# Two transformer blocks on one core: shift section behind the first taps, joined roots of two norms, another order of head pairs

## The reference

```python
sh1, sc1, g1, sh2, sc2, g2 = ada_terms(cond_lat, ada_w[i], ada_b[i])   # silu(c) @ w + b, six sections of 1024
hl = modulate(rmsnorm(x, norm1_g[i]), sh1, sc1)
yl = short_conv_mixer(hl, conv_w_in[j], conv_w[j], conv_w_out[j], True)
x = x + g1 * yl
x = x + g2 * swiglu(modulate(rmsnorm(x, norm2_g[i]), sh2, sc2), ffn_w_in[i], ffn_w_out[i])
return rmsnorm(x, final_g)
```

```python
h = _swiglu(_rmsnorm(x, g[0]), ...);  x = x + 0.5 * _rmsnorm(h, g[1])
h = mixer(_rmsnorm(x, g[2]));         x = x + _rmsnorm(h, g[3])
h = _swiglu(_rmsnorm(x, g[4]), ...);  x = x + 0.5 * _rmsnorm(h, g[5])
```

## Time and profile before

| | |
|---|---|
| median of 3 runs | 1320.87 us (1317.85 to 1321.43) |
| profiled execution, its own time | 1321.67 us |
| its span, first to last instruction | 1319.8 us |
| busy: DVE, ACT, POOL | 59%, 52%, 11% |
| mean TensorE clock granted | 0.994 of full |
| HBM read | 249.77 MB, 190 GB/s over the span |
| chain that ended last, by engine | PE 89%, DVE 4%, ACT 2% |

### The profile page before, as it was taken

How to read it: one execution, slowest core, us unless ns; L and a number is a source line. 1 busy time by engine, 2 the same in 40 slices (tenths; PEclk the granted TensorE clock), 3 DMA queues, 4 the chain that set the end, 5 groups by cost and what they waited for, 6 DMA issues and landing times.

```text
span 1319.8 us, 18568 instructions
## 1 busy us (share of the span) xinstructions
PE 1291.3 (98%) x6815; PEld 1064.7 (81%) x6815; DVE 781.8 (59%) x1023; ACT 687.9 (52%) x1035; POOL 139.5 (11%) x126
## 2 busy tenths in 40 slices
PE   8989999999999999999999999999999999999997
PEld 7877788887788888877888888888887897788886
DVE  4485666444755555666755556655556676755554
ACT  4453544444644445646644446544446656744443
POOL 3080097001600000020000000000000100000000
PEclk9999999999899999999999999999999999999999
DMA  9996386555455556572555554655563543555561
GB/s 338 378 373 207 123 302 213 188 183 186 160 179 184 182 187 215 171 205 64 189 184 184 184 202 157 209 183 184 188 225 126 162 151 119 189 186 183 183 205 57
DMA packets 177379, 253.64 MB, mean 192 GB/s; under 512 B 9352, under 2 KB 143796, under 8 KB 177332
## 3 DMA queue, kind: packets, MB, share of 16 engines
q1 hardware_dynamic: 174368, 244.33, 55.2%
q0 software_dynamic: 2624, 8.48, 1.7%
q10 hardware_dynamic: 340, 0.18, 0.1%
HBM read 249.77 MB, written 1.05 MB: 190 GB/s over the span
## 4 chain that ended last, share of the span: by engine, by line
PE 89%; DVE 4%; ACT 2%; DMA 1%; SPq 1%; POOL 1%; issue 1%; DVEq 0%; ACTq 0%; POOLq 0%
PE ps L598 26%; PE ps L600 25%; PE ps L599 25%; PE ps L638 2%; PE ps L639 2%; PE ps L683 2%; PE ps L646 2%; POOL arena L2198 1%; PE ps L1008 1%; PE ps L622 1%; DVE arena L1915 1%; DMA arena<-in_ada_w 1%; DMA raw<-in_conv_w_in 1%; PE ps L880 1%; SPq L477 1%; PE ps L869 1%
## 5 line engine op out<-in xcount | busy, mean ns | idle before, releaser
L1646 DVE TENSOR_TENSOR w_lo<-raw,w_hi 128x2048 fp32r<-128x2048 f32 x111 | 263.6, 2375 | 168.5 <-ACT w_hi L1182 168.5
L598 PE MATMUL ps<-w_lo,xT_hi 128*128 128x512 f32 x836 | 332.8, 398 | 3.0 <-DVE act_pair L1800 3.0
L600 PE MATMUL ps<-w_hi,xT_lo 128*128 128x512 f32 x836 | 327.5, 392 | 0.0
L599 PE MATMUL ps<-w_hi,xT_hi 128*128 128x512 f32 x836 | 327.2, 391 | 0.0
L1651 DVE SCALAR_TENSOR_TENSOR w_lo<-raw,par,w_hi 128x512 fp32r<-128x512 f32 x336 | 230.9, 749 | 135.1 <-ACT w_hi L1187 135.0
L1182 ACT ACTIVATE w_hi<-raw 128x2048 fp32r<-128x2048 f32 x111 | 212.1, 1912 | 143.6 <-PE ps L600 140.1
L1187 ACT ACTIVATE w_hi<-raw,par 128x512 fp32r<-128x512 f32 x336 | 214.3, 712 | 0.8 <-PE ps L600 0.8
L598 PEld LDWEIGHTS ps<-w_lo,xT_hi 128*128 128x128 f32 x836 | 157.8, 189 | 35.6 <-DVE act_pair L1800 3.5
L600 PEld LDWEIGHTS ps<-w_hi,xT_lo 128*128 128x128 f32 x836 | 157.7, 189 | 33.7
L599 PEld LDWEIGHTS ps<-w_hi,xT_hi 128*128 128x128 f32 x836 | 158.0, 189 | 31.6 <-issue 0.2
L598 PE MATMUL ps<-w_lo,hT_hi 128*128 128x512 f32 x400 | 156.7, 392 | 0.0
(11 more groups left out here) (248 smaller groups left out, 1527.6 us busy)
## 6 DMA issues: line engine op xcount, KB each, us to landing
raw<-in_ffn_w_gate SPq DMA_DIRECT2D x88, 512.0 KB, 3.7
raw<-in_ffn_w_up SPq DMA_DIRECT2D x88, 512.0 KB, 4.6
raw<-in_ffn_w_down SPq DMA_DIRECT2D x88, 512.0 KB, 4.0
raw<-in_ffn_w_in SPq DMA_DIRECT2D x44, 512.0 KB, 4.6
raw<-in_conv_w_in SPq DMA_DIRECT2D x24, 512.0 KB, 9.1
raw<-in_fox_w_in SPq DMA_DIRECT2D x24, 512.0 KB, 4.4
raw<-in_ffn_w_out SPq DMA_DIRECT2D x22, 512.0 KB, 4.1
raw<-in_ab_w_in SPq DMA_DIRECT2D x14, 512.0 KB, 4.4
```

What stands on the lines that cost most here:

```text
L598: pe.matmul(o, a_hi, b_lo, start=first, stop=False, skip_group_check=True)
L599: pe.matmul(o, a_hi, b_hi, start=False, stop=False, skip_group_check=True)
L600: return pe.matmul(o, a_lo, b_hi, start=False, stop=last, skip_group_check=True)
L1646: dve.tensor_tensor(w_lo[:, slot_of(n), :], raw[:, slot_of(n), :], w_hi[:, slot_of(n), :].bitcast(F32), ALU.subtract).then_inc(raw_done, 1)
```

## The change

There are three parts, in three places of the program.

**First mixer.** POOL's first load of the shift section waits for `evac_v` 2, that is for DVE's `conv_out(0)`. ACT multiplies the pieces later: `split(n + 7)`, `middle_taps(0)`, `split(n + 8)`, `conv_hi(0)` and `split(n + 9)` now stand ahead of `ada_times(0)`. On DVE `conv_out(0)` stands behind `split(n + 8)`. PE runs `shift_columns` behind units 10 and 11 and `mod_piece(6)`.

The diff, without the new semaphores and the lines that only rename; the lines of the orders above are left out:

```diff
@@ PE, AB @@
+            pair_part(n + 6, 0, 5)
             pe.wait_ge(evac_a, 9)
             pe.wait_ge(k_landed, 32)
             scores(AB, 0)
             scores(AB, 1)
-            pair_part(n + 6, 0, 5)
             pair_part(n + 6, 1, 5)
-            turn_probs(AB, 0)
             pe.wait_ge(tap_w_ok, 1)
             pe.wait_ge(rep_landed, 256)
             long_conv(0)
+            turn_probs(AB, 0)
+            long_conv(1, (0, TAPM // 2))
             head_outputs(AB, 0)
             turn_probs(AB, 1)
-            long_conv(1)
+            long_conv(1, (TAPM // 2, TAPM))
...
             turn_probs(AB, 3)
+            pe.wait_ge(oT_ok, 3)
+            down_part(n + 8, yT_hi, yT_lo, 6, 0, False, False, ks=(0,))
             head_outputs(AB, 3)
...
             pe.wait_ge(oT_ok, 4)
-            down_part(n + 8, yT_hi, yT_lo, 6, 0, False, False)
+            down_part(n + 8, yT_hi, yT_lo, 6, 0, False, False, ks=(1,))
@@ ACT, between(FFN0) @@
+                def summed_square(t):
+                    c = 2 * FINAL_EVENT + t
+                    act.wait_ge(x_mid, 2 * t + 2)
+                    act.activation(tmp[:, t, :], x[:, t, :], ACT.Square, scale=D ** -0.5,
+                                   accum_out=stat[:, 0, c:c + 1]).then_inc(x_sq, 1)
+                def gained_square(t):
+                    c = 2 * x_event(s) + t
+                    act.wait_ge(gained, t + 1)
+                    act.wait_ge(x_sq, 2 * FINAL_EVENT + t + 1)
+                    act.activation(tmp[:, t, :], xn[:, t, :], ACT.Square, scale=D ** -0.5,
+                                   accum_out=stat[:, 0, c:c + 1]).then_inc(gain_sq, 1)
...
-                        after(0)
+                        summed_square(0)
+                        gained_square(0)
                         split(n + 1)
                         turned_hi(s, 1)
-                        after(1)
-                        before(0)
-                        before(1)
+                        summed_square(1)
+                        gained_square(1)
+                        c, f = 2 * x_event(s), 2 * FINAL_EVENT
+                        act.wait_ge(x_sq, f + 2)
+                        act.activation(stat[:, 1, f:f + 2], stat[:, 0, f:f + 2], ACT.Sqrt, bias=eps[:, 0:1]).then_inc(x_std, 2)
+                        act.wait_ge(both_sq, 1)
+                        act.activation(stat[:, 1, c:c + 2], stat[:, 2, c:c + 2], ACT.Sqrt).then_inc(x_std, 2)
@@ DVE @@
+            def joined_roots():
+                c, f = 2 * x_event(FFN1), 2 * FINAL_EVENT
+                dve.wait_ge(x_sq, f + 2)
+                dve.wait_ge(gain_sq, 2)
+                link(dve.tensor_scalar(stat[:, 1, c:c + 2], stat[:, 0, f:f + 2], EPS, EPS * EPS, ALU.mult, ALU.add))
+                dve.tensor_tensor(stat[:, 2, c:c + 2], stat[:, 1, c:c + 2], stat[:, 0, c:c + 2], ALU.add).then_inc(both_sq, 1)
+                dve.wait_ge(x_std, f + 2)
+                dve.reciprocal(stat[:, 2, f:f + 2], stat[:, 1, f:f + 2]).then_inc(x_rstd, 2)
+                dve.wait_ge(x_std, c + 2)
+                dve.reciprocal(stat[:, 2, c:c + 2], stat[:, 1, c:c + 2]).then_inc(x_rstd, 2)
...
-            conv_out(0)
             split(n + 8)
+            conv_out(0)
@@ POOL @@
             pool.wait_ge(mod_ps, 4)
-            load_ada_p(0)
-            load_ada_p(1)
             pool.memset(half_sum, 0.0).then_inc(sum_cleared, 1)
             pool.wait_ge(sum_cleared, 2)
             sum_rows(half_sum, GATE1)
+            pool.wait_ge(evac_v, 2)
+            load_ada_p(0)
+            load_ada_p(1)
...
+            for t in range(TOKT):
+                pool.wait_ge(x_mid, 2 * t + 2)
+                pool.tensor_tensor(xn[:, t, :], x[:, t, :], rows[:, 1, :], ALU.mult).then_inc(gained, 1)
+
             pool.wait_ge(ada_ps, 5)
-            pool.wait_ge(x_new, x_count(CONV, 0, 0))
+            pool.wait_ge(x_rstd, 2 * x_event(FFN1) + 2)
```

More of the change, by code:

```diff
@@ L311, in block_program @@
         x_mid = sem("x_mid")
+        gained = sem("gained")
+        gain_sq = sem("gain_sq")
+        both_sq = sem("both_sq")
         gain_ok = sem("gain_ok")
@@ L1002, in _, with long_conv @@
             pair_part(n + 5, 1, 4)
-            def long_conv(c):
-                for m in range(TAPM):
+            def long_conv(c, ms=(0, TAPM)):
+                for m in range(*ms):
                     for q in range(4):
@@ L1434, in _ @@
             gate_out(0)
-            ada_times(0)
             split(n + 7)
             middle_taps(0)
-            ada_times(1)
             split(n + 8)
             conv_hi(0)
+            split(n + 9)
+            ada_times(0)
+            ada_times(1)
+            split(n + 10)
+            gate_out(1)
+            split(n + 11)
             ada_times(2)
-            split(n + 9)
-            gate_out(1)
+            middle_taps(1)
+            split(n + 12)
             ada_times(3)
-            split(n + 10)
-            split(n + 11)
+            split(n + 13)
+            conv_hi(1)
             act.wait_ge(ada_ps, 2)
             act.activation(mod[:, 0, :], ps[:, 1, 0:KT], ACT.Copy).then_inc(ada_row_a, 1)
-            middle_taps(1)
-            split(n + 12)
-            split(n + 13)
-            conv_hi(1)
             split(n + 14)
@@ L1703, in residual @@
                     o.then_inc(x_mid if b == FFN0 else x_new, 1)
+            def joined_roots():
[8 more added lines that the diff above has]
+                dve.reciprocal(stat[:, 2, c:c + 2], stat[:, 1, c:c + 2]).then_inc(x_rstd, 2)
             def final_x(t):
-                r = rms_x(FINAL_EVENT, t)
+                f = 2 * FINAL_EVENT + t
                 for h in range(2):
                     c = slice(h * 512, (h + 1) * 512)
-                    dve.scalar_tensor_tensor(x[:, t, c], x[:, t, c], r, rows[:, 1, c], ALU.mult, ALU.mult).then_inc(x_new, 1)
-            def joined_root(t):
-                c, f = 2 * x_event(FFN1) + t, 2 * FINAL_EVENT + t
-                dve.wait_ge(x_std, c + 1)
-                link(dve.reciprocal(stat[:, 0, c:c + 1], stat[:, 1, c:c + 1]))
-                dve.tensor_tensor(stat[:, 2, c:c + 1], stat[:, 0, c:c + 1], stat[:, 2, f:f + 1], ALU.mult).then_inc(x_rstd, 1)
+                    dve.tensor_scalar(x[:, t, c], xn[:, t, c], stat[:, 2, f:f + 1], None, ALU.mult).then_inc(x_new, 1)
             def norm_x(s, t):
@@ L1764, in between @@
                     residual(b, 1)
-                    final_x(0)
                     turned_lo(s, 1)
-                    final_x(1)
-                    for t in range(TOKT):
-                        joined_root(t)
+                    split(n + 1)
+                    joined_roots()
                 elif s in FOLDED:
@@ L1779, in between @@
                     residual(b, 1)
-                if s < 8:
+                if s < 8 and b != FFN0:
                     split(n + 1)
@@ L1818, in ffn @@
                 chunk(0)
+                if s == FFN1:
+                    for t in range(TOKT):
+                        final_x(t)
                 if s == FFN2:
@@ L1942, in _ @@
             outer_taps(0)
+            split(n + 8)
             conv_out(0)
-            split(n + 8)
             conv_lo(0)
```

18 lines of the change are left out of this document (8 added, 10 removed).

## The result

The changed kernel takes 1325.97 us, median of 5 runs (1324.08 to 1327.55), against 1320.87 us before. Its ratio to before is 1.0039, 95% interval 1.0027 to 1.0051, so it is slower by about 5 us. Medians and ratios here leave out two slow executions, one of the kernel before (1667.62 us, mean clock 0.722) and one of e4 (1845.37 us, 0.654). The forecast of 1318.8 us and its range (to 1325) are missed. What came is the mechanism of the late chain, whose figure was 1325.9 us. The profiled execution took 1325.51 us (span 1323.8), 3.8 more than the profiled one of before.

What follows compares the result with a forecast made beforehand. PE was taken to bound the kernel, busy for 1291.3 of 1319.8 us. First mixer +1.5, FFN0 to FFN1 -2.4 and AB -1.2 sum to -2.1 us, so 1318.8 us against the median; range 1311.5 to 1325.

Steps and rivals of the forecast that it cites:

- late chain: Rival, first mixer: four serial pieces end last, PE stands over 3 us, clock falls, +5.8 there; 1325.9 us, chance 0.17.
- First mixer +1.5: First mixer: the output product starts at 117.7 us instead of 116.19, costing 1.5 us; ends -3.0 and +5.8.
- Lands 7.6 us later: First mixer: piece 4 of the shift section lands 7.6 us after its issue.
- by then SyncE has little left to load: First mixer: argument against the late chain, that piece 4 lands as in the 7.6 us row.
- my later end of 117.6: First mixer: latest time put for the end of POOL's additions of piece 4, range 112.0 to 117.6 us.
- the 117.7 which I took: First mixer: start of PE's output product, taken from a range of 114.0 to 119.6 us.
- the upper end: First mixer: slow end, +5.8 us, output product at 119.6 to 120.4 and another 1.6 us of low clock.
- The second way to the same point: First mixer: DVE's path to the output product through unit 13's split and conv_out(1), 112.4 to 116.2, or 117.4 if blocked.
- FFN0 to FFN1 -2.4: FFN0 to FFN1: 0.3 us lost at PE's going on, 2.7 regained from the clock, -2.4 us; ends -5.3 and +0.6.
- AB -1.2: AB: reordering covers PE waits of 2.0 us, about 0.7 comes back, -1.2 us; ends -2.0 and +0.3.

Runs made afterwards that it cites:

- e4: Changed kernel with small fill products on PE in its two stalls, ahead of mod_piece(4) and the shift columns: 1325.09 us, ratio 1.0029.
- e11: Changed kernel with one 1 MB load on SP's queue (load_mod(7)) moved behind the two weight loads that follow it: 1322.62 us, ratio 1.001.
- e6: Changed kernel with unit 10's split ahead of piece 2's multiplication on ACT: 1326.11 us, ratio 1.0029.
- e7: Changed kernel with piece 4 of the first mixer's shift section cut to 8 of 1024 columns (load, multiplications, additions): 1316.87 us, ratio 0.9962.
- e1: Changed kernel with its first-mixer part undone, keeping the joined roots and the new AB order: 1319.14 us, ratio 0.998.
- e8: Kernel before, with 12 fill products on PE where it waits 3.05 us in FFN1: 1320.62 us, ratio 0.9995.
- e2: Kernel before with only the first-mixer part of the change: 1330.43 us, ratio 1.0061.
- e9: Changed kernel with pieces 1 and 2 loaded early, multiplications and second taps moved earlier, and 12 fill products ahead of the shift columns: 1315.91 us, ratio 0.9957.

## Why the prediction was wrong

**The step that failed is "First mixer +1.5".** It was +10.5 at the turn for FFN0, 9.0 more. Two of its terms made most of that: the landing of piece 4, put at 7.6 us and measured at 11.3, and the clock, put at nothing and measured at 4.3 us. The mechanism was named rightly, and so were the first links: loads free at 73.3 (I had 73.7), piece 1 multiplied at 86.9 (86.1), piece 1 added at 91.8 (91.1), piece 2 added at 99.7 (97.2 to 101.0), piece 4 issued at 99.95. First taps in 3.25 us and no wait near 80, as said.

*The transfer.* "Lands 7.6 us later" was read from one row of before. The argument beside it, "by then SyncE has little left to load", was the error. Around that row SP issued nothing from 71.7 to 84.1 us. In the changed kernel DVE's and ACT's splits stood still while ACT waited for piece 1 (8.8 us) and multiplied; DVE's next split ended at 97.40, and only then did a buffer come free for SP. Its issues from 74 to 110 us:

```profile
78.28 0.81 SPq L432 DMA_DIRECT2D raw<-in_conv_w_out  x2
79.14 0.43 SPq L489 DMA_DIRECT2D rows<-in_ada_w  x1
97.43 0.80 SPq L432 DMA_DIRECT2D raw<-in_conv_w_out  x2
98.28 0.43 SPq L489 DMA_DIRECT2D tmp<-in_ada_w  x1
101.83 7.97 SPq L432 DMA_DIRECT2D raw<-in_conv_w_out  x4
```

Nothing from 79.6 to 97.4 us, then 2 MB just ahead of piece 4. e11 shows that this matters: one load moved, and piece 4 lands in 5.9 us. The forecast took a duration from a row without taking the neighbours of that row. The additions ended at 120.36, 2.8 past my later end of 117.6: 3.7 for the transfer and 0.5 for issue and start gaps, less 1.35 since piece 2 was added that much before my later figure. Against the 115.75 that is in the 117.7 which I took, it is 4.6.

*The clock.* The forecast's own times held a long wait of PE ahead of the columns. It had PE at the output product at 110.0 without stalls, so at the columns at 108.05, or at 110 to 112 behind the first wait of 2 to 4 us, and the additions at 115.75: a wait of 3.7 to 5.7 us (5.4 was measured). Its own rows had half clock behind waits of 3.9 and 3.0 us. Yet the +1.5 has nothing for the clock, only the upper end has 1.6, and the prediction's last sentence calls the forecast wrong if PE waits over 3 us anywhere in these places. In the changed kernel the output product started 3.43 us behind the start of the columns, where I had 1.95, so 1.5 later, and the output product ran 10.3 us at half clock, which cost 2.8 (24 products in 8.48 us, before in 5.67). Of the 9.0 us, then, the chain made some 4.7, 3.7 of them the transfer, and the clock 4.3.

That the transfer alone doesn't repair the forecast is shown by e11 and e6. Both had it below my 7.6 us (5.9 and 6.9), and both were above the forecast (1322.62 and 1326.11 us, against 1318.8); e11's turn for FFN0 came at 148.11, or 146.8 against PE's course, 5.2 us later than before and not 1.5. e7 shows that the transfer, the clock behind the second wait and the additions all hang on the fourth link.

The second way to the same point was worked out rightly as a path (`conv_out(1)` 112.4 to 116.2, or 117.4), but it too hangs on piece 4, through unit 13's split behind the multiplication, and ended at 119.3. In e11, with the fast transfer and the taps blocked as in my 117.4, it ended at 121.0, or 119.7 against PE's course. That the stall ahead of `mod_piece(4)` costs nothing as long as the chain ends later fits e6, though that run moved the chain as well; the stall was 4.7 us, not 2 to 4.

One more thing was wrong in it. The second taps ran free (3.25 us) in the changed kernel, where I said they would run slow; the additions came too late to meet them. They did meet once the chain was shortened (7.48 and 7.66 us). The Trainium skill, "SBUF — State Buffer", section "Who interferes with whom", says that such a DVE instruction and a GpSimd instruction that reads SBUF exclude each other. By that rule the traces agree: 3.25 us with no addition beside the taps, 7.66 with two.

**"FFN0 to FFN1 -2.4"** was right in kind and somewhat small. Between the turn for FFN0 and that for AB the offset falls by 5.2 us, but 1.4 of it is not the change's: before, the clock fell at FFN0's start, and in this execution it didn't (185.70 us from the turn to PE's last wait in FFN0 against 184.32; e1, with the new roots, has 185.70 too). Of the remaining 3.8, PE's going on behind `hidden` gives 1.0 (I had 0.3 lost), and the clock 2.85 (I took 2.7; e8 measures 2.87 by itself, but e2's execution of the old order lost only 1.4). The predicted order was there. The first POOL product blocked a DVE split (3.55 us for two instructions), and the second hardly touched one, whence the better 1.0:

```profile
343.24 3.55 DVE L1694 SCALAR_TENSOR_TENSOR w_lo<-raw,par,w_hi 128x512 fp32r<-128x512 f32 x2
...
353.80 2.99 DVE L1675 SCALAR_TENSOR_TENSOR w_lo<-raw,par,w_hi 128x512 fp32r<-128x512 f32 x4
```

**"AB -1.2"** was right: from turn to turn 469.94 us instead of 471.15, that is 1.2 less, with one wait of 0.5 us for L1578 and none for the scores. e1, with the new order, has 470.01; e2 and e8, with the old one, have 471.08 and 471.12.

**The chances.** The late chain had 0.17. Each link was worked out, but both ends took 7.6 us for the last transfer, while the profile also held 10.2 and 14.6 us; with 10.2 in the sum the output product comes to 120.3, past the 119 from which the late chain was to decide. By its own split the chances add to 0.48 for the same and 0.17 for slower, not 0.47 and 0.18.

**What stays open.** How e11's one moved megabyte shortens a transfer by 5.4 us, when its bytes make 2.6, isn't shown, nor what an 8 KB transfer waits for during 6.8 us; nor why the clock falls at FFN0's start in some of these executions and not in others.

## What to carry to other kernels

Before work is moved to start later, look for buffers that make it a chain: four pieces through two buffers are two trips in a row, each with its landing time. Take a transfer's time from a moment with the same neighbours in the queues, and ask which loads the move itself delays into it. Then ask whether the consumer must stand where it stands: with the chain already shortened, moving the columns 24 products back on PE, together with `conv_out(1)` ahead of one split, gave another 5 us.

## What was not expected of the hardware

A transfer of 1 MB on POOL's queue landed after anything between 5.6 us (e2, issued at 92.1, with nothing else moving) and 15.7 us (e6) in these mixers. The two that were issued together in the changed kernel, at 73.3 and 74.1 us:

```profile
arena<-in_ada_w POOLq DMA_DIRECT2D x1, 1024.0 KB, 11.3
xn<-in_ada_w POOLq DMA_DIRECT2D x1, 1024.0 KB, 15.4
```

The clock doesn't answer to the pattern of waits alone. FFN0's start has the same three waits of PE in every kernel here (0.4, 0.9 and 2.0 us); behind them the clock was at 0.62 in the kernel before (150 to 154 us), and at 1.00 in the changed one (160 to 164). The same wait of 3.05 us in FFN1 cost 6.4 us at half clock before, and in e2 (3.06 us) a stretch with 0.75 on the mean:

```profile
362.00:368.40 6.40, 6.12 (x21) 4.98 (x22) 5.61 (x7) 2.80 (x3) 1.05 (x3) 0.75 0.69 205
```

Such falls are worth 1 to 3 us each, about what the runs of one kernel differ by, so a gain in the clock at one place (e4, e8, e9) shows in the trace and not in the median.
